# Even layer of a 512-token transformer kernel: the compression's hidden activations in one slot, the forget attention's halves made sooner, and one transposed pack copied between two groups of row maxima

## The reference, cut to what matters

```python
def even_mixer(h, ...):
    ...
    o_fox = fox_attention(heads(fq, 8), heads(fk, 8), heads(fv, 8), log_f)   # forget attention, 8 heads, causal
    o_nsa = nsa_attention(
        rope(heads(nq, 8)),
        compress(rope(heads(kc, 2)), cpk, c1k, c2k),     # 31 blocks of 32 tokens -> hidden 128 -> 64
        compress(heads(vc, 2), cpv, c1v, c2v),
        rope(heads(ksl, 2)), heads(vsl, 2),              # selected branch
        rope(heads(kwn, 2)), heads(vwn, 2),              # window branch
        jax.nn.sigmoid(gl).reshape(B, T, 8, 3))
    o = jnp.concatenate([o_fox, o_nsa], axis=-1)
    return o @ w_out

def compress(x, pos, w1, w2):
    blocks = x[:, idx] + pos
    ...
    return jax.nn.gelu(flat @ w1) @ w2
```

## Time and profile before

| | |
|---|---|
| median of 3 runs | 2333.71 us (2333.36 to 2337.08) |
| profiled execution, own time / span | 2332.5 us / 2330.5 us |
| PE busy | 2202.0 us, 94% |
| PE weight load busy | 1785.1 us, 77% |
| DVE busy | 1239.7 us, 53% |
| ACT busy | 1120.4 us, 48% |
| POOL busy | 726.8 us, 31% |
| chain that ended last, by engine | PE 79%, DVE 7%, ACT 7%, issue 4%, POOL 2% |
| mean granted TensorE clock | 0.977 of full speed |

### The profile page before, as it was taken

How to read it: one execution, slowest core, us unless ns; L and a number is a source line. 1 busy time by engine, 2 the same in 40 slices (tenths; PEclk the granted TensorE clock), 3 DMA queues, 4 the chain that set the end, 5 groups by cost and what they waited for, 6 DMA issues and landing times.

```text
span 2330.5 us, 30231 instructions
## 1 busy us (share of the span) xinstructions
PE 2202.0 (94%) x10952; PEld 1785.1 (77%) x10952; DVE 1239.7 (53%) x2212; ACT 1120.4 (48%) x1964; POOL 726.8 (31%) x479
## 2 busy tenths in 40 slices
PE   8899999989999999988989999999989899999997
PEld 6676677767888887766868888887877777888886
DVE  6776575558999634455455232234467455332223
ACT  6456554457888635555354322224676344332222
POOL 4261233410000221510344332324742434333233
PEclk9989999999999999998999999999999999999999
DMA  4402233217999630220222223231311221322221
GB/s 167 149 28 68 73 102 110 74 73 289 392 389 389 229 100 20 72 91 1 82 72 68 95 100 100 91 101 66 102 58 37 73 73 55 101 99 97 97 96 55
DMA packets 74531, 264.13 MB, mean 113 GB/s; under 512 B 8272, under 2 KB 8400, under 8 KB 74000
## 3 DMA queue, kind: packets, MB, share of 16 engines
q1 hardware_dynamic: 66816, 238.76, 29.2%
q0 software_dynamic: 2816, 11.82, 1.4%
q10 hardware_dynamic: 4752, 11.61, 1.4%
HBM read 247.98 MB, written 14.18 MB: 112 GB/s over the span
## 4 chain that ended last, share of the span: by engine, by line
PE 79%; DVE 7%; ACT 7%; issue 4%; POOL 2%; DMA 1%; POOLq 0%; DVEq 0%; ACTq 0%; SPq 0%
PE ps L518 17%; PE ps L520 17%; PE ps L519 17%; PE ps L1171 3%; PE ps L582 2%; PE ps L2896 2%; PE ps L2898 2%; PE ps L2897 2%; PE ps L1186 2%; PE ps L1205 2%; PE ps L564 1%; ACT Sb L1292 1%; PE ps L2923 1%; PE ps L558 1%; PE ps L2924 1%
## 5 line engine op out<-in xcount | busy, mean ns | idle before, releaser
L454 ACT ACTIVATE wh<-raw 128x1024 fp32r<-128x1024 f32 x308 | 322.3, 1054 | 443.6 <-PE ps L520 415.0
L459 DVE TENSOR_TENSOR wl<-raw,wh 128x1024 fp32r<-128x1024 f32 x176 | 235.5, 1344 | 506.1 <-ACT wh L454 499.2
L459 POOL TENSOR_TENSOR wl<-raw,wh 128x1024 fp32r<-128x1024 f32 x132 | 318.7, 2415 | 492.1 <-ACT wh L454 483.7
L518 PE MATMUL ps<-hh,wh 128*128 128x512 f32 (+1 forms) x1192 | 468.0, 393 | 0.3 <-DVE wl L459 0.3
L519 PE MATMUL ps<-hl,wh 128*128 128x512 f32 (+1 forms) x1192 | 464.5, 390 | 0.0
L520 PE MATMUL ps<-hh,wl 128*128 128x512 f32 (+1 forms) x1192 | 464.4, 390 | 0.0
L518 PE MATMUL ps<-act,wh 128*128 128x512 f32 (+1 forms) x688 | 268.9, 391 | 12.9 <-ACT act L1448 9.9
L519 PE MATMUL ps<-act,wh 128*128 128x512 f32 (+1 forms) x688 | 267.2, 388 | 0.0
L520 PE MATMUL ps<-act,wl 128*128 128x512 f32 (+1 forms) x688 | 267.1, 388 | 0.0
L518 PEld LDWEIGHTS ps<-hh,wh 128*128 128x128 f32 (+1 forms) x1192 | 223.7, 188 | 49.1 <-issue 2.4
L520 PEld LDWEIGHTS ps<-hh,wl 128*128 128x128 f32 (+1 forms) x1192 | 223.6, 188 | 47.5 <-issue 0.4
(11 more groups left out here) (471 smaller groups left out, 3915.9 us busy)
## 6 DMA issues: line engine op xcount, KB each, us to landing
raw<-d_w SPq DMA_DIRECT2D x277, 512.0 KB, 3.2
raw_x<-d_moe SPq DMA_DIRECT2D x84, 512.0 KB, 6.5
raw<-d_moe SPq DMA_DIRECT2D x84, 512.0 KB, 6.7
d_xs<-Sb POOLq DMA_DIRECT2D x7, 514.0 KB, 7.6
Xb<-d_xs ACTq DMA_DIRECT2D x6, 514.0 KB, 6.5
area<-d_mem POOLq DMA_DIRECT2D x3, 1024.0 KB, 5.2
d_ys<-rows ACTq DMA_DIRECT2D x6, 512.0 KB, 5.7
xT<-d_x SPq DMA_DIRECT2D x8, 256.0 KB, 6.1
```

Source lines behind the costliest of these rows:

```text
L454: me.e.activation(hi, raw, ACT.Copy).then_inc(*me.done("wh", m))
L459: me.e.tensor_tensor(lo, raw, hi.bitcast(F32), ALU.subtract).then_inc(*me.done("wl", m))
L518: me.e.matmul(bank[0:m, 0:n], wh[:, c], hi, start=k == 0, stop=False)
```

## The change

Three edits, all of them in the order of instructions; nothing is computed otherwise.

1. In the attentions with a second set of buffers, DVE makes copy 0 directly behind the first group of maxima, ahead of the output of pair s - 2 and of the second group. Copy 1 stays where it was. This holds for DSA, fox, NSA and the three memory attentions.
2. In `compressed_side` DVE finishes the GELU of both tiles (keys and values) in the first of the two slots.
3. `parts_of(... "of" ...)` is taken out of `even_out` and put into a function of its own, `even_forget_out`. ACT and DVE run it as `finish` in the last round of the NSA attention, ahead of the last pair's scales and output, and POOL behind the flush of its side work. Its wait is for the last score product alone. The halves "on" wait for PE's end, no longer for DVE's as a whole.

```diff
--- before.py
+++ after.py
@@ -1346,10 +1346,12 @@
     me.alias("end", "pe", a)
 
 
-def attention_act(K, me, a, items, first=(), pt_first=(), ticks=0):
+def attention_act(K, me, a, items, first=(), pt_first=(), ticks=0, finish=None):
     pairs = pairs_of(items)
     for step in range(len(pairs) + 2):
         p = step - 1
+        if finish and step == len(pairs) + 1:
+            finish(K, me)
         if step > 1:
             scales_act(K, me, a, p - 1, pairs[p - 1][0])
         me.tick(ticks)
@@ -1363,7 +1365,7 @@
     me.alias("end", "act", a)
 
 
-def attention_dve(K, me, a, items, first=(), pt_first=(), ticks=0, weights=None):
+def attention_dve(K, me, a, items, first=(), pt_first=(), ticks=0, weights=None, finish=None):
     pairs = pairs_of(items)
     for step in range(len(pairs) + 2):
         p = step - 1
@@ -1375,6 +1377,10 @@
             sums_dve(K, me, a, p, pairs[p])
         if step < len(pairs):
             max_dve(K, me, a, step, pairs[step][0], 0, first)
+        if 0 <= p < len(pairs) and K.second[a]:
+            turned_copy(K, me, a, p, pairs[p][0], 0, pt_free(a, p, pt_first))
+        if finish and step == len(pairs) + 1:
+            finish(K, me)
         if step > 1:
             out_dve(K, me, a, p - 1, pairs[p - 1][0])
         if step < len(pairs):
@@ -1383,8 +1389,7 @@
             ahead(K, me, weights)
         me.tick(ticks)
         if 0 <= p < len(pairs) and K.second[a]:
-            for h in range(2):
-                turned_copy(K, me, a, p, pairs[p][0], h, pt_free(a, p, pt_first))
+            turned_copy(K, me, a, p, pairs[p][0], 1, pt_free(a, p, pt_first))
             sums_dve(K, me, a, p, pairs[p])
         me.tick(ticks)
     me.alias("end", "dve", a)
@@ -3468,10 +3473,13 @@
         u = a[0:2 * NCMP, 18, 256 * s + 128:256 * s + 256]
         ht = K.mis[:, 96 + 64 * s:96 + 64 * s + 62]
         if me.name == "dve":
-            me.wait_ge("cmp", "tanh", s)
-            e.tensor_scalar(u, u, 0.5, 0.5, ALU.mult, ALU.add).then_inc(*me.done())
-            me.wait_ge()
-            e.tensor_tensor(hs, hs, u, ALU.mult).then_inc(*me.done("cmp", "hact", s))
+            for r in range(2) if s == 0 else ():
+                hr = a[0:2 * NCMP, 18, 256 * r:256 * r + 128]
+                v = a[0:2 * NCMP, 18, 256 * r + 128:256 * r + 256]
+                me.wait_ge("cmp", "tanh", r)
+                e.tensor_scalar(v, v, 0.5, 0.5, ALU.mult, ALU.add).then_inc(*me.done())
+                me.wait_ge()
+                e.tensor_tensor(hr, hr, v, ALU.mult).then_inc(*me.done("cmp", "hact", r))
             me.wait_ge("hidt", s)
             e.tensor_copy(ht, K.bank("hidt", s)[:, 0:2 * NCMP]).then_inc(*me.done("cmp", "hb", s))
         if me.name == "pe":
@@ -3616,16 +3624,22 @@
     heads_act(K, me, "nsa", K.i_nsa, "n3", 0)
     values_act(K, me, "vsw", K.i_vsw)
     me.beside = compressed_side(K, me)
-    attention_act(K, me, "nsa", K.i_branch, [("end", "pe", "fox")], [("pv", "fox", 3)], ticks=2)
+    attention_act(K, me, "nsa", K.i_branch, [("end", "pe", "fox")], [("pv", "fox", 3)], ticks=2,
+                  finish=even_forget_out)
     me.flush()
     me.alias("end", "act", "nsa")
     even_out(K, me)
     sandwich_act(K, me, "x4", "n4", "mem1")
 
 
+def even_forget_out(K, me):
+    last = len(pairs_of(K.i_branch)) - 1
+    parts_of(K, me, "of", 4, 0, lambda c: K.area[:, 20 + c, :], [("whole", "of", c) for c in range(4)],
+             [("S", "nsa", last, 1, 1)])
+
+
 def even_out(K, me):
-    war = [("end", "pe", "nsa"), ("end", "dve", "nsa")]
-    parts_of(K, me, "of", 4, 0, lambda c: K.area[:, 20 + c, :], [("whole", "of", c) for c in range(4)], war)
+    war = [("end", "pe", "nsa")]
     parts_of(K, me, "on", 4, 8, lambda c: K.O[:, c, :], [("cmp", "add", c) for c in range(4)], war)
 
 
@@ -3641,7 +3655,8 @@
     values_dve(K, me, "vsw", K.i_vsw, norm="n3")
     me.beside = compressed_side(K, me)
     K.o_last = [("out", "nsa", c) for c in range(4)]
-    attention_dve(K, me, "nsa", K.i_branch, [("end", "pe", "fox")], [("pv", "fox", 3)], ticks=2)
+    attention_dve(K, me, "nsa", K.i_branch, [("end", "pe", "fox")], [("pv", "fox", 3)], ticks=2,
+                  finish=even_forget_out)
     me.flush()
     me.alias("end", "dve", "nsa")
     even_out(K, me)
@@ -3677,6 +3692,7 @@
     attention_pool(K, me, "nsa", K.i_branch, ticks=2)
     me.flush()
     me.alias("end", "pool", "nsa")
+    even_forget_out(K, me)
     even_out(K, me)
     mem_load(K, me, "mem1")
     sandwich_pool(K, me, "x4", ("x", "x3"), "n4", "mem1")
```

## The result

Four runs of the changed kernel took 2353.78 to 2364.71 us, with a median of 2360.04; the four of before have a median of 2334.43. The ratio is 1.009, interval 1.0069 to 1.0111 (the quotient of the two medians is 1.0110): slower, as forecast, and by more than forecast (2349.7). The median lies 1.0 us above the upper end of the stated range; the ratio times the median of before is 2355.4. The profiled execution took 2358.13 us, 25.6 more than the profiled one of before.

The account below looks back on a forecast made before the run. PE, 94% busy, bounds the kernel through when DVE reaches instructions it waits for. Losses +23.0, gains -7.7 and clock +0.7 gave +16.0 us: 2348.5 profiled, median 2349.7; own range 2345 to 2355, 8-in-10 range 2341 to 2359.

Parts of the forecast that it names:

- DSA, forecast +3.9: DSA's steps with scores of pairs 1 to 3: copy 0's wait delays the maximum freeing the late pack's bank, +3.9 us.
- Fox, forecast +5.3: Fox's steps with scores of pairs 1 to 3: the bank-freeing maximum comes late by 1.4, 2.0, 2.0 us; +5.3 us.
- the term of 0.7 us for the clock: Slower matmuls behind the new PE gaps: +0.7 us, range 0 to 8.
- rival C: Clock falls in fox, DSA and NSA's late steps: 8 us instead of 0.7, time 2357 us; chance 0.15.
- NSA, forecast +8.9: NSA's share of the forecast's sum, with the gain from the joint GELU included: +8.9 us.
- Pairs 1 to 3: NSA's steps with these scores: same wait, partly covered by PE's side work; +0.5, +1.0, +0.5, together +2.0 us.
- Edit 2: NSA's step with pair 4's scores: PE's 3.85 us wait for the second tile's GELU goes; -3.6 us.
- Pairs 5 and 6: NSA: DVE stands before copy 0, delaying second group, softmax blocks and ACT's copies; +7.0 us, bounds 1.7 and 8.
- Pair 7: NSA's step with pair 7's scores: copy, two output instructions and two maxima delay pack 2 of head 0; +3.5 us.
- Edit 3, forecast -4.1: Output projection: PE's 3.64 us gap and slow first matmuls shrink through fox's early halves; -4.1 us, bounds -5.4 and -2.5.
- rival D: End of NSA: fox's early halves make the last addition 2.2 us later, gain only -1.9, time 2351.9; chance 0.08.
- Memory attentions, forecast +1.3: Last round of the three memory attentions: PE waits for the output behind copy 0; 0.4 us each, +1.3 us.

Follow-up runs that it names:

- e1: Changed kernel with copy 0 put back behind the second group and side work, so only joint GELU and fox's early halves; ratio 0.9976 to the kernel before.
- e5: Kernel before with only the early copy 0, and that in DSA alone; ratio 1.0027 to the kernel before.
- e6: Kernel before with only the early copy 0, and that in fox alone; ratio 1.0023 to the kernel before.
- e8: Kernel before with the early copy 0 in NSA alone, plus the GELU of both tiles in one slot; ratio 1.0056 to the kernel before.
- e9: Changed kernel with copy 0 behind the third maximum of the second group, the one that frees the bank; ratio 1.0004 to the kernel before.
- e2: Changed kernel without fox's early halves (early copy 0 and joint GELU kept); ratio 1.0115 to the kernel before.
- e7: Early copy 0 in fox alone, with fox's output of pair s - 2 moved behind the second group of maxima; ratio 1.0017 to the kernel before.
- e3: Kernel before with only the GELU of both tiles in one slot; ratio 0.9992 to the kernel before.
- e4: Kernel before with only fox's early halves; ratio 0.9981 to the kernel before.
- e12: As e11, with DVE's two low halves of fox behind the last output instead of ahead; ratio 0.9943 to the kernel before.
- e11: Joint GELU and fox's early halves, no early copy 0, output of pair s - 2 behind the second group's third maximum; ratio 0.9947 to the kernel before.
- e10: Changed kernel with copy 0 behind the whole second group, ahead of the side work; ratio 0.9977 to the kernel before.

## Why the prediction was right or wrong

**Direction and mechanism: right.** Everything that DVE has ahead of the second group moves PE, since the late pack goes into a bank of those scores. e1 removes the copy and all loss, e5, e6 and e8 give the losses back stage by stage, e9 leaves the copy between the maxima but behind the one in question and has hardly a loss in DSA (0.4) and none in fox.

**DSA, forecast +3.9: measured +4.0** in the changed kernel, e2 and e5.

**Fox, forecast +5.3: +5.32 where the clock stayed up (e2), +7.1 where it fell.** PE came 1.4, 2.0 and 2.0 us later in its three steps (idle rows of 1.27, 1.87 and 1.87), as forecast. What failed is the term of 0.7 us for the clock, which I set near its low end "since most of the new gaps are shorter than 2.33". The clock fell behind gaps of 1.87 in two of three profiles with that order, and in e7 behind 1.27 and 0.47. In DSA the same 1.87 left the clock at 1.00 in the changed kernel. That is rival C in part. In fox it is 1.8 us of the 9.6 by which the profiled pair exceeds the forecast.

**NSA, forecast +8.9 in all (with edit 2): measured +13.2, e8 +13.4, e2 +10.4.** By stretches of the trace of before:

- Pairs 1 to 3 (984 to 1030 before): forecast 2.0, measured 1.5 (e8 1.8, e2 3.2), where kernels without edit 1 in NSA move by -2.1 to +0.3.
- Edit 2 (1030 to 1045): forecast -3.6, measured -2.9 (-4.7 and -4.8 in e1 and e3, so edit 1 takes 1.9 of it back). From 1045 to 1056, where no term was forecast, the changed kernel gains another 1.3.
- Pairs 5 and 6 (1056 to 1083): forecast 7.0, measured 10.3; e8 10.3, e2 8.3; kernels without edit 1 in NSA move by -2.7 to 0.0 there. The path was the forecast one to the row: idle DVE, second group, two softmax blocks, ACT's exponential, ACT's copies; ACT began its copies 10.0 us behind the start of the transposes, forecast 10.0, and PE came 6.5 us later to the first product, forecast 6.4. What was missing is that the products then ran at half clock (3.22 us for six, 1.72 before), which adds 2.9 us.
- Pair 7 (1083 to 1101): forecast 3.5, measured 5.5 in the changed kernel with a gap of 3.36, 2.8 in e2 with the same gap. The wait is 3.3 of it, near the forecast; the other 2.3 are the clock once more: the products take 2.61 for five after it, 1.40 before.

**Edit 3, forecast -4.1: measured -3.06 at the first matmul of the projection in six kernels, and -3.1 to -3.3 at the end of the first output tile (1111.6 before), to which the forecast reckoned.** The gap went but for 0.58 us. The forecast also counted on 1.8 us from slow matmuls at full speed and on NSA's halves at 1106.4, and in no kernel did both come. In the changed kernel the first nine matmuls still run at half speed (0.43 us apart, 0.23 later) behind that gap of 0.58, and PE waits for nothing after them. In e4 they run at full speed, and PE then waits for the first half of NSA's last output:

```profile
1112.63 0.47 PE L518 MATMUL ps<-act,wh 128*128 128x512 f32 x1 [1.23 <-ACT act L1452]
```

That wait is the late last addition: it starts 3.4 us behind the end of PE's last matmul of NSA in the changed kernel and in e4, and 1.3 before, because DVE's two low halves of fox (1.28 at 1128.66) stand ahead of the output and one addition beside POOL's half took 1.54 us at 1130.58 instead of 0.69. These 2.1 us are rival D's 2.2, but the gain did not shrink to D's 1.9. The cure that I tried (e12) is worse: the halves are needed sooner than the output.

**Memory attentions, forecast +1.3: +0.8 where the forecast put it.** Over the whole stretch of the first one (456 to 510 before) nothing can be told: it moved by +2.3, but by +1.7 in e1 and +2.9 in e3, which have no edit there. In the last round itself, from the last transpose to the spread sums behind the products, PE is 0.26 us later in each of the three, in the changed kernel and in e2, and 0.0 in all other kernels. It is the wait that was forecast, PE's for the output:

```profile
1231.10 1.94 PE L1205 MATMUL ps<-PT,sel 128*64 128x512 f32 x8 [0.51 <-DVE O L1415]
```

**The sum.** Forecast +16.0 against the profiled run, measured +25.6. Of the 9.6 between them, 4.3 are NSA, 1.8 fox, 1.0 edit 3, 0.1 DSA, and 2.4 the other stretches: 4.4 measured (0-283, 304-887, the rest), where kernels without the edit move as much, less the 1.3 forecast for the memory attentions and the 0.7 for the clock. The step that failed is the size of the clock's term, 0.7 us: in the changed kernel's profile slow matmuls behind the new gaps cost 1.8 in fox, 2.9 in the step of pair 5 and 2.3 in that of pair 7, together 7.0, near the upper bound of 8. In e2's profile they cost 1.8 in the step of pair 5 and 1.5 behind a gap of 2.57 among pairs 1 to 3, and nothing in fox and pair 7. The waits of DSA, fox, pair 5 and pair 7 came out within 0.3 us of the forecast. That the ratio nevertheless gives a time inside the range (2355.4) owes something to the width of the range, since this term was off by a factor of ten in the profiled execution. The Trainium skill, "TensorE: Matmul & The Clock Gate", part 1, says that the throttled state is the default and that activity releases it; it does not say that every gap is followed by slow matmuls, as the prediction's strict reading of it had. That strict reading agrees with the traces in fox in three profiles and in NSA, and not in DSA, nor in fox in e2.

## What to carry to other kernels

Before an instruction is moved up in an engine's queue, look at what it waits for, not at how long it takes: a copy of 0.47 us cost 1.1 to 6.5 us of waiting a step, because its wait went in front of work that another engine needed sooner. Where buffers rotate, the instruction that frees a buffer is what has to come first, and the consumer of the moved result tells whether being early buys anything at all; here it did not. Add to the waits what the clock may do behind the new gaps; in this kernel that was 7.0 us in the changed kernel's profile and 3.3 in e2's. In a trace the place to look is an idle of PE ended by DVE that ends a constant time (here 0.57 us) after the start of one particular instruction; e11 shows that moving work behind that instruction gains where there is such a gap (DSA, 1.5 us), and costs where there is none (fox, 0.6).

## What the runs showed of the hardware that was not expected

The clock behind a gap did not follow from the gap alone: the same order of fox with gaps of 1.27, 1.87 and 1.87 us ran at 1.00 in e2 and at 0.93 in the changed kernel. DSA with gaps of 1.66, 1.87 and 1.87 stayed at 1.00 in three profiles (changed kernel, e2, e5). A clock that fell added 1.8 us in fox, 2.9 in NSA's step of pair 5, and 2.3 in that of pair 7.

DVE's addition with two inputs in SBUF took 1.54 us while a POOL tensor operation ran (DVE L1423 at 1130.58 beside POOL L1459 at 1130.29 to 1131.57), 0.69 for the same addition with POOL idle (e12, 1098.67). It took 1.53 to 1.56 us in the same place in e1, e4, e9, e10 and e11. The additional 0.85 us fell on the path to the last addition; PE waited behind it in e4 alone.
